# Low-rank gate projection in a two-layer hybrid trunk: one f32 product in column tiles, or split fp32r products

## What is computed

```
z = rmsnorm(h, norm_mix_pre) @ w_in              # 1024 -> 3104 columns
x_br, gate_br, q, k, v, g_out, zg_f, zg_b = split(z, [512, 512, 256, 256, 512, 512, 16, 16])
y_lru = rglru_group(x_br, gate_br, ...)           # conv, gates, two scans
g_f = log_sigmoid(zg_f @ wg_f + bg_f) / 16        # 16 -> 256 columns, forward decays
g_b = log_sigmoid(zg_b @ wg_b + bg_b) / 16        # and backward
y_gla = gla(q, k, v, g_f, g_b) ...                # chunked linear attention
h = h + rmsnorm(concat(y_lru, y_gla) @ w_out, norm_mix_post)
h = h + rmsnorm(relu(rmsnorm(h, norm_mlp_pre) @ w_up)**2 @ w_down, norm_mlp_post)
```

## Time and profile before

| | kernel before |
|---|---|
| time, median of 3 runs | 2238.58 us |
| time of the profiled execution | 2238.58 us |
| its span in the trace | 2236.8 us |
| TensorE busy | 2202.9 us, 98% |
| VectorE busy | 1621.2 us, 72% |
| ScalarE busy | 862.7 us, 39% |
| GpSimd busy | 387.5 us, 17% |
| TensorE matmul records | 13856 |
| TensorE's granted clock, mean | 0.997 |

### The profile page before, as it was taken

How to read it: one execution, slowest core, us unless ns; L and a number is a source line. 1 busy time by engine, 2 the same in 40 slices (tenths; PEclk the granted TensorE clock), 3 DMA queues, 4 the chain that set the end, 5 groups by cost and what they waited for, 6 DMA issues and landing times.

```text
span 2236.8 us, 34155 instructions
## 1 busy us (share of the span) xinstructions
PE 2202.9 (98%) x13856; PEld 2002.2 (90%) x13856; DVE 1621.2 (72%) x1638; ACT 862.7 (39%) x996; POOL 387.5 (17%) x217
## 2 busy tenths in 40 slices
PE   8999999999999999999999999999999999999997
PEld 6999989999999999999989999877788888888887
DVE  6788635576877977977587886354768779778858
ACT  4564423352333342331254653242524433433412
POOL 3433214112000000002414332151130000000050
PEclk9999999999999999999999999999999999999998
DMA  3111103265653554551241111022666554654523
GB/s 142 34 55 37 38 20 95 73 209 208 234 188 144 208 183 171 176 189 67 88 144 48 53 39 38 20 95 68 214 213 230 195 181 149 244 186 140 181 67 142
DMA packets 122803, 291.01 MB, mean 130 GB/s; under 512 B 9552, under 2 KB 29264, under 8 KB 122704
## 3 DMA queue, kind: packets, MB, share of 16 engines
q1 hardware_dynamic: 56688, 166.24, 21.3%
q10 hardware_dynamic: 66016, 123.38, 16.2%
HBM read 251.51 MB, written 38.08 MB: 129 GB/s over the span
## 4 chain that ended last, share of the span: by engine, by line
PE 87%; DVE 8%; ACT 2%; issue 2%; DMA 0%; DVEq 0%; POOL 0%; SPq 0%; ACTq 0%; POOLq 0%
PE banks L757 31%; PE banks L997 20%; PE banks L1027 19%; PE banks L888 5%; PE banks L809 3%; PE banks L812 1%; PE banks L1127 1%; PE banks L797 1%; PE banks L796 1%; PE banks L1134 1%; PE banks L1083 1%; PE banks L1104 1%; PE banks L1142 1%; PE banks L926 0%; DVE sum_lo L2285 0%
## 5 line engine op out<-in xcount | busy, mean ns | idle before, releaser
L757 PE MATMUL banks<-X,w_hl 128*128 128x348 f32 (+2 forms) x3744 | 649.4, 332 | 2.4 <-ACT ki L1514 1.8
L757 PEld LDWEIGHTS banks<-X,w_hl 128*128 128x128 f32 x3744 | 606.2, 188 | 29.1 <-issue 5.3
L660 POOL TENSOR_SCALAR w_hl<-w_raw 128x1024 fp32r<-128x1024 f32 x70 | 82.2, 1174 | 1717.4 <-PE banks L1027 954.2
L997 PE MATMUL banks<-X,w_hl 128*128 128x260 f32 (+1 forms) x1944 | 311.6, 319 | 0.0
L1027 PE MATMUL banks<-sum_hi,w_hl 128*128 128x260 f32 (+1 forms) x1440 | 310.9, 320 | 0.0
L997 PEld LDWEIGHTS banks<-X,w_hl 128*128 128x128 f32 x1944 | 277.8, 188 | 29.0 <-DVE Y L2236 0.4
L1027 PEld LDWEIGHTS banks<-sum_hi,w_hl 128*128 128x128 f32 x1440 | 223.9, 188 | 21.5
L662 POOL TENSOR_TENSOR w_hl<-w_raw,w_hl 128x1024 fp32r<-128x1024 f32 x70 | 206.3, 2947 | 5.8
L1027 PE MATMUL banks<-sum_lo,w_hl 128*128 128x260 f32 (+1 forms) x720 | 191.0, 319 | 0.0
L1613 ACT ACTIVATE sum_hi<-hid 128x1040 fp32r<-128x1040 f32 (+1 forms) x72 | 76.8, 1066 | 206.3 <-PE banks L1027 206.3
L2299 DVE TENSOR_TENSOR Y<-banks,Y 128x520 f32<-128x520 f32 (+1 forms) x144 | 122.2, 867 | 26.4 <-PE banks L1027 25.9
(11 more groups left out here) (244 smaller groups left out, 3610.0 us busy)
## 6 DMA issues: line engine op xcount, KB each, us to landing
w_raw<-w_units SPq DMA_DIRECT2D x148, 512.0 KB, 3.5
r<-w_units SPq DMA_DIRECT2D x82, 512.0 KB, 4.1
X<-t_mem ACTq DMA_DIRECT2D x44, 520.0 KB, 5.3
X<-t_mem ACTq DMA_DIRECT2D x44, 512.0 KB, 4.9
X<-t_mem SPq DMA_DIRECT2D x28, 520.0 KB, 5.4
X<-t_mem SPq DMA_DIRECT2D x28, 512.0 KB, 5.4
t_extra<-t_mem ACTq DMA_DIRECT2D x16, 520.0 KB, 4.4
t_extra<-t_mem ACTq DMA_DIRECT2D x16, 512.0 KB, 5.0
```

The lines of the kernel that those rows point to most:

```text
L660: nc.gpsimd.tensor_scalar(slot[:, 0], w_raw[:, s], 1.0, 1.0, ALU.mult, ALU.mult).then_inc(w_rounded, 1)
L757: ins = nc.tensor.matmul(out[:, b, 0:t.width(b)], wp, xp[:, t.used(b)], start=first and n == 0, stop=last and n == 2)
L997: ins = nc.tensor.matmul(banks[:, first + b, 0:t.block], wp, xp[:, b * t.block:(b + 1) * t.block], start=opens and (half, kk, i) == (0, 0, ...
```

## The change

The gain no longer goes into zg's weights. GpSimd splits them, as it does the others, into a rounded half and a rest (`zg_hl`, fp32r), which stand beside each other as 64 columns of one weight tile. TensorE multiplies these 64 columns by the high half of X and then by the low half, for each channel tile and block: 8 x 2 x 3 = 48 fp32r matmuls in a layer, all into partitions 0 to 63. The result is two partial sums of 32 rows each, one from the weights' rounded half and one from the rest. VectorE scales 64 rows into `acc`, and the decay products contract 64 rows rather than 128, with two copies of the decay weights.

```diff
-        decay_w = sb("decay_w", [128, 512])
+        decay_w = sb("decay_w", [4 * RANK, 512])
...
-        zg_w = sb("zg_w", [128, 8, 2 * RANK])
+        zg_hl = sb("zg_hl", [128, 8, 2, 2 * RANK], f32r)
...
                 pool.wait_ge(zgw_loaded, 16 * (l + 1))
                 pool.sem_inc(waited_pool, 1)
-                gain = par[:, l, P_GMIX:P_GMIX + KT].unsqueeze(2).to_broadcast([128, KT, 2 * RANK])
-                nc.gpsimd.tensor_tensor(zg_w[:, :, :], zg_raw[:, :, :], gain, ALU.mult).then_inc(zgw_ready, 1)
+                nc.gpsimd.tensor_scalar(zg_hl[:, :, 0], zg_raw[:, :, :], 1.0, 1.0, ALU.mult, ALU.mult).then_inc(zgw_step, 1)
+                pool.wait_ge(zgw_step, l + 1)
+                nc.gpsimd.tensor_tensor(zg_hl[:, :, 1], zg_raw[:, :, :], zg_hl[:, :, 0].bitcast(f32), ALU.subtract)\
+                    .then_inc(zgw_ready, 1)
...
                     ins = nc.tensor.matmul(ps(J_W[n])[:, b, 0:FULL.width(b)], decay_w[:, n * 128:(n + 1) * 128],
-                                           acc[:, FULL.used(b)], start=True, stop=True)
+                                           acc[0:4 * RANK, FULL.used(b)], start=True, stop=True)
...
                 take_set(l, J_ZG)
-                columns = 128 // (2 * RANK)
-                for k0 in range(0, KT, columns):
-                    for b in range(NB):
-                        for c in range(columns):
-                            rows = slice(2 * RANK * c, 2 * RANK * (c + 1))
-                            ins = nc.tensor.matmul(ps(J_ZG)[rows, b, 0:FULL.width(b)], zg_w[:, k0 + c, :], Y[:, k0 + c, FULL.used(b)],
-                                                   start=k0 == 0, stop=k0 + columns == KT, skip_group_check=True)
+                for k in range(KT):
+
+                    for n, xp in enumerate(xtile(k)):
+                        for b in range(NB):
+                            ins = nc.tensor.matmul(ps(J_ZG, 4 * RANK)[:, b, 0:FULL.width(b)], zg_hl[:, k].rearrange("p h n -> p (h n)"),
+                                                   xp[:, FULL.used(b)], start=k == 0 and n == 0, stop=k == KT - 1 and n == 1)
                 ins.then_inc(mm_done, 1)
...
-                scaled_out(l, J_ZG, 0, done(l, J_ZG), blk(acc[:, :]))
+                scaled_out(l, J_ZG, 0, done(l, J_ZG), blk(acc[0:4 * RANK, :]), rows=4 * RANK)
...
-    w_decay = np.zeros((L, 128 // (2 * RANK), 2 * RANK, 512), np.float32)
+    w_decay = np.zeros((L, 2, 2 * RANK, 512), np.float32)
```

More of the change, by code:

```diff
@@ L442, in trunk_kernel @@
         w_ready = sem("w_ready")
-        zgw_loaded, zgw_ready = sem("zgw_loaded"), sem("zgw_ready")
+        zgw_loaded, zgw_step, zgw_ready = sem("zgw_loaded"), sem("zgw_step"), sem("zgw_ready")
         gatew_loaded, gates_hi, gates_ready = sem("gatew_loaded"), sem("gates_hi"), sem("gates_ready")
```

## The result

The changed kernel takes 2251.91 us, the median of 6 runs (2248.29 to 2253.41), against 2238.57 for the kernel before in the same runs (2237.94 to 2239.94). The ratio is 1.0056 with a 95% interval of 1.0046 to 1.0065. It is slower, as forecast, but by 13.3 us and not by 7.8, and the time lies outside the range, which ended at 2248.6. The profiled execution took 2251.31 us.

A forecast was written before the change was run, and what follows sets the result against it. TensorE, with an instruction under way in 98% of the span, was taken to bound the kernel. Terms +7.97 - 0.77 + 0 + 0.6 = +7.8 us took 2238.58 to 2246.4 us, range 2243.6 to 2248.6.

The forecast's parts named there:

- the path: Whole kernel: TensorE's order sets the time, so what the zg stage gains or loses is handed on to the end.
- the zg stage: zg products on TensorE, each layer: 48 matmuls at 0.160 us take 7.69 us instead of about 3.70, together +7.97 us.
- the stall's end: First LRU gate job, both layers: TensorE comes 4 us later, finds its inputs ready and no longer waits, -0.77 us.
- So height does not enter: 0: Decay products: contracting 64 rows rather than 128 changes nothing, 0 us, judged from attention's 64-row and 104-row matmuls.
- A loss has no reason: Decay products: dismissal of any slowdown from 64 rows, beside a possible -7.0 us that no row pointed to.
- GpSimd's term: Second layer's start: GpSimd's two zg-weight instructions delay VectorE, on which TensorE waits, +0.6 us (bounds 0 and +1.3).
- the other figure that the prediction gives, 0.8: Same place: by the Trainium skill's SBUF lockout rule, the sum for GpSimd's instructions would be +0.8 us rather than +0.6.
- the split between the two instructions: Same place: rounding costs VectorE 0.24 us as the old instruction did; subtraction holds the second update up for 0.62 us.

The follow-up runs named there:

- after_again: The changed kernel measured once more with no edit: 2252.3 us (2251.0 to 2252.92), ratio 1.0055 against the kernel before.

## Why the prediction was wrong

What held: the path (TensorE hands on what it loses: the second layer's stages lie where the first one's delays put them), the zg stage (0.161 us a matmul against 0.160, 7.73 and 7.74 us against 7.69), and most of the stall's end (0.66 of 0.77 us; for the rest, the load path now stands idle 0.19 us ahead of the second gate job, until VectorE has read v). Weights of 64 columns load in 134 ns, on the line of the others, and the stage is within 0.05 us of the forecast one.

The step that failed is the one on the decay products, "So height does not enter: 0". It compared the durations of attention's matmuls with 64 and with 104 rows. A duration tells what one instruction takes once it runs. It doesn't hold what is lost between it and its neighbours, and the 64-row matmuls of attention stand in packs of 8 and 16, so that their medians say nothing of the borders. The decay products' own medians are alike too, 454 ns with 128 rows and 452 with 64. What the runs showed in place of the 0 is 0.39 us for each decay product, +3.14 us in all: 1.94 for 1.75 us in the stage, and 0.2 in the run behind it, which two edits took out (128 rows in the changed kernel) and put in (64 rows in the kernel before). "A loss has no reason" was wrong too. The trace of the kernel before had shown the price. Its chain from 264 to 286 us, and the form of L1104's weights (64 rows by 104 columns):

```profile
273.26 1.43 PE banks L757 x9
274.69 1.02 PE banks L1083 x16
275.71 0.57 PE banks L1071 x4
276.28 0.91 PE banks L1104 x16
277.20 1.61 PE banks L757 x9
278.81 1.02 PE banks L1083 x16
279.83 1.64 PE banks L757 x9
281.47 0.91 PE banks L1104 x16
```
```profile
L1104 PEld LDWEIGHTS banks<-qi,ki 64*104 64x104 f32 x320 | 16.2, 167 | 10.4 <-issue 9.2 <-DVE ki L2123 1.2
```

Nine matmuls of the same unit take 1.43 us everywhere else in this stretch, but 1.61 behind the 64-row products and 1.64 ahead of the next ones. Ahead of L1083, whose weights have 64 columns but 104 rows, they keep 1.43, so it is the rows and not the columns. That is the 0.2 us to either side. With 8 products it gives 8 x 0.4 = 3.2 us, and the forecast would have been 2249.6. That is within the changed kernel's runs, though still 2.3 us below their median.

GpSimd's term was too large: +0.24 where 0.6 was taken, and the other figure that the prediction gives, 0.8, was further off. The place was right and the split between the two instructions wrong. Before, the multiplication cost the first update 0.24 us (0.82 and 0.57 us for the two, 0.58 each undisturbed). The forecast let the rounding cost the same again and the subtraction 0.62 more. By the rows above, the first update is as short as undisturbed (0.59), since the rounding ran mostly beside VectorE's multiplication ahead of them, which ends at 1124.02, and only the second is held up, by 0.47 us (1.05), beside the subtraction. The two together take 1.57 us where they took 1.31.

The other 1.9 us of the profiled pair (1.6 + 0.5 - 0.2) come from the clock and the start, which vary from one execution to the next. What I can't settle: the medians differ by 12.5 us (after_again) and 13.3, the rows that belong to the code add up to 10.8 (8.06 - 0.66 + 3.14 + 0.24), and both edits of the decays alone moved the median by 4.3 rather than 3.1 us. The intervals allow for either. The stretch behind 1596 us varies by some 2 us between profiles, as shown above, which is enough to hide the difference. Profiles with 64-row decays may be more prone to the small waits there, but one profile each doesn't show that, and I did not find what decides when the clock falls.

## What to carry to other kernels

Count the borders between matmul shapes, not only the matmuls: when a stream of 128-row matmuls is broken by a few products of 64 rows, pad them to full height with zero rows, if the rows are free. To price an instruction that stands alone among others, read how long its neighbours take in the chain beside it and away from it; its own duration can be the same within 2 ns and the cost still be there. And where one f32 product in column tiles replaces a stream of narrow split ones, the tiles win: 3.7 us against 7.7 here, although by itself each f32 instruction is more than three times as dear (0.58 against 0.16 us).

## What was new about the hardware

Weights of 64 rows between weights of 128 cost about 0.2 us on each side, once for a group (1.94 us for 6 records and 3.69 for 12), while 96 rows cost nothing (1.75). The granted clock fell to the 1.2 GHz level behind a TensorE wait of 2.34 us in one execution of the changed kernel, and stayed up behind the same wait in another of the same code; it fell behind a wait of 1.86 us too, in the version with the early split. Where it fell, it cost 1.6 us.
